# Homes of the matmul operands in SBUF, moved by their address modulo 256

## The reference

```python
# first block
h = x
h = h + gated_deltanet(rmsnorm(h, a_norm), ...)        # x @ w_in, delta rule per head, @ w_out
h = h + conv_ffn(rmsnorm(h, f_norm[0]), ...)           # @ w_up, conv of 3 taps, silu(gate) * val, @ w_down
kv = rmsnorm(h, kv_norm) @ w_kv
h = h + chunk_attention(rmsnorm(h, b_norm), w_q, ...)  # banded attention, @ w_out
h = h + conv_ffn(rmsnorm(h, f_norm[1]), ...)
x = rmsnorm(h, final_norm)
# second block, with 256 context tokens
h, hc = modulate(rmsnorm(x)), modulate(rmsnorm(ctx))   # shifts, scales, gates from c @ w_mod
# h @ w_in, hc @ w_in, retention and attention
x = x + g1 * (concat(ret, att) @ w_out)
x = x + g2 * (square(relu(modulate(rmsnorm(x)) @ w_ff1)) @ w_ff2)
return rmsnorm(x, final_norm_g)
```

## The kernel before

| buffer | role in the split product | before | after |
|---|---|---|---|
| xH, xL | streams and is loaded | 0 | 224 (-32) |
| yH, yL | streams; yH is loaded as zH | 64 | 160 (-96) |
| zL | loaded | 64 | 0 |
| x2H, x2L | streams and is loaded | 64 | 32 |
| xcH, xcL | loaded | 64 | 96 |
| aH, aL | loaded | 64 | 0 |
| cst (identity) | streams in transposes | 160 | 128 |
| xn, feat, T_, p_b, ap_ and others of `place` | in matmuls of plain float32 and transposes | 64 | 0 |

## Time and profile before

### The profile page before, as it was taken

How to read it: one execution, slowest core, us unless ns; L and a number is a source line. 1 busy time by engine, 2 the same in 40 slices (tenths; PEclk the granted TensorE clock), 3 DMA queues, 4 the chain that set the end, 5 groups by cost and what they waited for, 6 DMA issues and landing times.

```text
span 1127.7 us, 20436 instructions
## 1 busy us (share of the span) xinstructions
PE 1057.8 (94%) x7432; PEld 967.6 (86%) x7432; DVE 856.3 (76%) x1538; ACT 590.2 (52%) x1011; POOL 89.6 (8%) x105
## 2 busy tenths in 40 slices
PE   3999999899999999999999999999999779999995
PEld 2998998799999879988999998888767669998884
DVE  4899888869888878775798888768777474557764
ACT  4556523456666446475766665455454554445441
POOL 0103323110000000000000001002000100000000
PEclk9999999899999999999999999999999889999998
DMA  8476333477665786735676668734312064666852
GB/s 248 127 203 187 100 114 106 124 227 211 186 186 186 250 272 198 251 113 194 172 228 186 184 184 297 226 93 149 102 56 76 1 195 123 184 186 214 260 180 75
DMA packets 216942, 193.25 MB, mean 171 GB/s; under 512 B 6896, under 2 KB 194416, under 8 KB 216752
## 3 DMA queue, kind: packets, MB, share of 16 engines
q1 hardware_dynamic: 206832, 159.24, 47.3%
q0 software_dynamic: 8864, 33.05, 8.7%
q10 hardware_dynamic: 1184, 0.14, 0.1%
HBM read 191.35 MB, written 1.06 MB: 171 GB/s over the span
## 4 chain that ended last, share of the span: by engine, by line
PE 77%; DVE 9%; issue 6%; ACT 4%; DMA 2%; POOL 1%; DVEq 0%; SPq 0%; POOLq 0%; ACTq 0%
PE ps L560 23%; PE ps L561 23%; PE ps L562 23%; DVE cv L1902 2%; DVE wL L1880 1%; DMA raw<-in_a_w_in 1%; DMA raw<-in_f_w_up 1%; ACT wH L1159 1%; PE ps L992 1%; PE ps L970 1%; PE ps L812 1%; PE ps L674 1%; PE ps L722 1%; ACT p_b L1409 0%; PE ps L853 0%
## 5 line engine op out<-in xcount | busy, mean ns | idle before, releaser
L1159 ACT ACTIVATE wH<-raw 128x1024 fp32r<-128x1024 f32 x298 | 309.8, 1058 | 236.7 <-PE ps L562 218.5
L1880 DVE TENSOR_TENSOR wL<-raw,wH 128x1024 fp32r<-128x1024 f32 x298 | 355.8, 1220 | 76.2 <-ACT wH L1159 73.0
L560 PE MATMUL ps<-yH,wH 128*128 128x256 f32 x704 | 197.2, 280 | 0.7 <-DVE wL L1880 0.7
L561 PE MATMUL ps<-yL,wH 128*128 128x256 f32 x704 | 197.0, 280 | 0.0
L562 PE MATMUL ps<-yH,wL 128*128 128x256 f32 x704 | 196.4, 279 | 0.0
L560 PE MATMUL ps<-xH,wH 128*128 128x256 f32 x512 | 146.0, 285 | 2.5 <-DVE xL L1880 2.4
L561 PE MATMUL ps<-xL,wH 128*128 128x256 f32 x512 | 145.6, 284 | 0.0
L562 PE MATMUL ps<-xH,wL 128*128 128x256 f32 x512 | 145.5, 284 | 0.0
L560 PEld LDWEIGHTS ps<-yH,wH 128*128 128x128 f32 x704 | 132.3, 188 | 1.0 <-DVE wL L1880 0.9
L561 PEld LDWEIGHTS ps<-yL,wH 128*128 128x128 f32 x704 | 132.2, 188 | 0.1
L562 PEld LDWEIGHTS ps<-yH,wL 128*128 128x128 f32 x704 | 131.7, 187 | 0.0
(11 more groups left out here) (395 smaller groups left out, 1911.8 us busy)
## 6 DMA issues: line engine op xcount, KB each, us to landing
raw<-in_f_w_up SPq DMA_DIRECT2D x88, 512.0 KB, 4.9
raw<-in_w_ff SPq DMA_DIRECT2D x64, 512.0 KB, 4.3
modw<-in_w_mod_t POOLq DMA_DIRECT2D x48, 512.0 KB, 4.7
raw<-in_f_w_down SPq DMA_DIRECT2D x44, 512.0 KB, 4.4
raw<-in_a_w_in SPq DMA_DIRECT2D x32, 512.0 KB, 4.9
raw<-in_w_in SPq DMA_DIRECT2D x22, 512.0 KB, 4.1
raw<-in_w_kv SPq DMA_DIRECT2D x16, 512.0 KB, 5.1
raw<-in_a_w_out SPq DMA_DIRECT2D x8, 512.0 KB, 3.5
```

The lines of the kernel that those rows point to most:

```text
L560: mm(o, l[0], r[0], start=first, stop=False, skip_group_check=check)
L561: mm(o, l[0], r[1], start=False, stop=False, skip_group_check=check)
L1159: fn(wH[:, c % SPLIT], raw[:, c % RAW], ACT.Copy).then_inc(hi_done, 1)
L1880: return tt(o, x, hi.bitcast(F32), ALU.subtract)
```

## The change

It adds gaps and moves pads, so that the homes change as in the table above. No instruction is added, removed or reordered. `gap_x` puts 224 bytes ahead of xH; with it everything behind shifts, and `gap_places` brings the base of all `place` calls and stacks level with the weights. Single buffers are then set off from that base by their pads or by gaps of their own. Some pads shrink by a quarter of a KiB or less, so that yH, row_f1 and aqT keep clear of what lies beside them.

```diff
         h = sb("h", [P, TT, D])
+        sb("gap_x", [P, 56])
         xH = sb("xH", [P, KD, SEQ], F32R)
         xL = sb("xL", [P, KD, SEQ], F32R)
...
+        sb("gap_places", [P, 56])
+
         def place(kib, *names):
 
             with ExitStack() as s:
                 if kib:
-                    sb(f"pad_{names[0][0]}", [P, kib * 256], where=s)
+                    sb(f"pad_{names[0][0]}", [P, int(kib * 256)], where=s)
                 return [sb(*n, where=s) for n in names]
...
-        yL, = place(22, ("yL", [P, KD, SEQ], F32R))
-        yH, = place(48, ("yH", [P, KD, SEQ], F32R))
-        row_f1, = place(44, ("row_f1", [P, D]))
-        ctx_in, xcH, xcL, xvc, wt, tb, rows_c = place(
-            56, ("ctx_in", [P, TT, D]), ("xcH", [P, KD, SEQ], F32R),
+        yL, = place(22.15625, ("yL", [P, KD, SEQ], F32R))
+        yH, = place(47.90625, ("yH", [P, KD, SEQ], F32R))
+        row_f1, = place(43.75, ("row_f1", [P, D]))
+        ctx_in, _, xcH, xcL, xvc, wt, tb, rows_c = place(
+            56, ("ctx_in", [P, TT, D]), ("gap_xc", [P, 24]), ("xcH", [P, KD, SEQ], F32R),
...
-        aqT, = place(44, ("aqT", [P, 4, SEQ]))
+        aqT, = place(43.75, ("aqT", [P, 4, SEQ]))
...
-            64, ("rqT", [P, RET_H, SEQ]), ("rkT", [P, RET_H, SEQ]), ("sT01", [P, 2, 512]), ("o_r", [P, TT, RET_H, P]),
+            64.09375, ("rqT", [P, RET_H, SEQ]), ("rkT", [P, RET_H, SEQ]), ("sT01", [P, 2, 512]), ("o_r", [P, TT, RET_H, P]),
...
-        s_fb, = place(81, ("s_fb", [P, 2, RET_H, P]))
-        sT3, = place(86, ("sT3", [P, 512]))
+        s_fb, = place(81.09375, ("s_fb", [P, 2, RET_H, P]))
+        sT3, = place(86.09375, ("sT3", [P, 512]))
...
-        modw2, = place(80, ("modw2", [P, MOD_RING, D]))
+        modw2, = place(80.09375, ("modw2", [P, MOD_RING, D]))
...
             vt = sb("vt", [P, TT, D], where=s)
+            sb("gap_x2", [P, 8], where=s)
             x2H = sb("x2H", [P, KD, SEQ], F32R, where=s)
             x2L = sb("x2L", [P, KD, SEQ], F32R, where=s)
```

## The result

The changed kernel takes 1123.81 us (median of 8 runs, 1121.8 to 1124.64), the kernel before 1129.82 (8 runs, 1125.25 to 1134.3). The ratio is 0.9941 [0.9925, 0.9957], 6.0 us less. The forecast was 1109.5 us, 20.8 less. The result lies inside the stated range of 1097 to 1127, near its upper end and near rival (b).

What follows compares the result with a forecast made beforehand. PE, busy 94% of the span, was taken as the bound through its matmuls' pitch. The terms summed to -20.8 us, from the profiled 1129.5 to 1108.7, with 0.8 added for the median: 1109.5 us, range 1097 to 1127.

Steps and rivals of the forecast that it cites:

- rival (b): Only the level pair counts: y keeps 117.7 ns, x keeps 120, only the activations gain; 1124.6 us, chance 0.12.
- What bounds the kernel: PE, busy 94% of the span, through a pitch that differs by up to 7 ns with homes' distance modulo 256.
- Term 1: Activations aH, aL loaded, distance -64 to 0: 912 matmuls of 512 columns from 233.3 to 227.1 ns, -5.7 us.
- Term 2: y streaming, distance +64 to -96: 2112 matmuls taken at 113.1 ns from 117.7, -9.7 us.
- Term 3: x streaming, distance 0 to -32: 1536 matmuls taken at the middle, 116.6 ns, -5.4 us.
- Term 4: x loaded under 256 columns, distance to +32: 720 matmuls at 118.9 ns, -0.9 us.
- Term 5: x loaded under 512 columns, distance to +32: 192 matmuls, taken at nothing, between -1.2 and +1.2 us.
- Term 6: x2 streaming +0.2 us, x2 loaded +0.3; second block's output product, a third going to the level pair, +0.4.
- Term 7: Context rows loaded under 512 columns, distance -64 to -96: taken at nothing, between -0.6 and 0.6 us.
- Term 8: Transposes through the identity (cst), mostly +96 to +128: taken at nothing, though 7 ns each would be some 2 us.
- (c): Slower: x goes up to 127 ns streamed and loaded, y at -96 to 120; +15.2, 1145.5 us, chance 0.11.
- (d): No effect: the program around the rows, not the home, makes them differ; 1130.3 us, chance 0.05.

Runs made afterwards that it cites:

- e2_only_acts: The kernel before with only the activation tiles aH, aL moved level with the weights: 1124.74 us, ratio to before 0.9949.
- the sweeps: Kernels with only PE's split product and copies, operands at sixteen homes, repeated 96 bytes higher in reverse order: 256 streamed columns took 113.3 to 120.0 ns.
- both moves: The changed kernel with x and y each 64 bytes below the weights: 1112.13 us, ratio to before 0.9835.

## Why the prediction was wrong

- **What bounds the kernel** held. PE's pitch decides, and each change of it came through: the waits of PE stayed, 0.6 us for wL. DVE's cover was right too: with x and y at 113.3 in part the wait for wL is 2.2 us in all.
- **Term 1** (activations, -5.7 us) was right: 227.0 ns, and 4.8 us by the medians of e2_only_acts. It was the one term with a row at both ends, and it is most of the measured gain. One sentence beside it was wrong: the DMA was not as busy in the two stretches of 512 columns, its share was 0.72 (225 GB/s) from 359 to 389 us and 0.35 (96 GB/s) from 768.5 to 779. That this didn't make the 6 ns is shown only by e2_only_acts and the sweeps.
- **Term 2** (y, -9.7 us) is the step that failed most: it is off by 9.1 us, where the whole forecast of -20.8 is off by 12.0 from the traces' -8.8. It took -96 to be as cheap as "nearest is -64, 113.1", and measured 117.4, -0.6 us. The row that it leaned on was of a loaded y under streamed weights. And near counts for nothing here: at 192 itself the streamed pitch is 113.3, 4 bytes off it is 118.9 or 120.1.
- **Term 3** (x streams, -5.4 us) read a value between two rows off a straight line: 116.6. It measured 118.3, -2.8 us.
- **Term 4** (x loaded, 256 columns, -0.9) was too small: 116.7, -2.4 us. **Term 5** (x loaded, 512 columns) was taken at nothing and cost +1.2, its upper bound: it went from the cheap 227 to 233, by the same step that term 1 gained.
- **Term 6** was too small: yH at +96 was left out and went from 113 to 118, as zL did; +0.9 us instead of +0.4, and x2 as loaded operand +0.6 instead of +0.3. Term 7, taken at nothing, lies within its bound (234.4 ns before, 234.7 after); 48 context matmuls of 256 columns, left out of it, went from 113.6 to 117.3, 0.2 us. Term 8 was nothing: transposes kept their 109 ns from start to start.
- The **rivals**: (b), term 1 alone at 1124.6 us and with a chance of 0.12, is what happened in sum, though not in its reason: x did gain, and other roles and the clock took some of it back. That the sum is so near is partly luck. (c) fails, no group went over 120 on average. (d) fails by e2_only_acts. The Trainium skill ("SBUF — State Buffer", Who interferes with whom) says that PE never waits on anyone. Read as a rule on PE's own two operands, which the page doesn't spell out, it would make the sweeps flat, and the trace disagrees: with all other engines at rest the same matmuls take 113.3 to 120.1 ns by the home of an operand. Whether the loading of the next tile is what the stream runs into was not tested by itself; that one pitch depends on the distance of the two is what is shown.
- The step that failed, in one sentence: I saw that the pitch depends on the distance and that history plays in, and then interpolated a function of which I had three points, where it has no smoothness at all: y at -96 measured 117.4 and not 113.1, x at -32 118.3 and not 116.6.

## What to carry to other kernels

Where PE bounds a kernel and loads a tile for every matmul, the homes of the streamed and the loaded operand modulo 256 are worth trying (1.7 to 1.9% here with both moves), but only as measured values: a sweep of PE alone gives the values that a home can take, the kernel showed the same ones, and a home 4 bytes off is another place. Which of two values a stretch gets the sweep doesn't tell. A buffer with several roles (streamed, loaded under 256, loaded under 512) needs each role weighed by its count, since a home that is good for one is often bad for another. And a pitch that changes between stretches of one program is to be read per stretch and over several executions before a term is built on it.

## What the runs showed of the hardware

- The pitch of a split-product matmul goes by the distance of its operands' homes modulo 256, takes certain values (113.3, 116.7, 117.8, 118.3, 120.0 ns among others for 256 columns; 226.7, 228.9, 233.3 for 512), and at 192 changes by 5 to 7 ns within 4 bytes. Why is open.
- At some distances one rhythm was seen (0: 120.0), at some two (-64: 113.3 or 117.8; -96: 117.3 or 118.7), with 144 streamed even three values (113.3, 116.7, 118.7). At -64 and -96 a draw lasted for a whole stretch, 750 to 950 matmuls without a break, and it differed between executions of one program; but y at +64 in the kernel before left 113.3 after some 45 matmuls for 117.7. One up projection's draw is worth 1056 x 4.5 ns = 4.8 us, so it can account for a part of the 5 to 10 us by which runs of one of these kernels differ; that wasn't tested, and the clock has a part too.
- The executions of the kernel before, 1123.9 to 1135.0 us, get longer as the mean granted clock falls from 0.984 to 0.973; one spell at the lower level made 1.7 us between the two profiles of the result.
- Streamed and loaded are not mirror images: home 64 loaded and home 192 streamed are the same distance and both can run at 113.3, but 112 streamed is 113.3 and 144 loaded, also the same distance, 118.3 or 120.0.
- DVE's work beside PE leaves the pitch alone: in the changed kernel the mean pitch of x's matmuls was 118.2 ns where DVE was idle and 118.4 beside DVE's subtraction that makes wL.
